# The down weights of a mixture of experts, loaded by halves of the partitions instead of halves of the rows

## The reference, cut to what matters

```
logits = h @ router_w + router_b
gates, top_i = softmax of the two largest logits, their experts
for e in range(8):
    g, u = split(h @ w_gu[e])               # w_gu[e]: 1024 x 7168
    y += combine[:, e] * ((silu(g) * u) @ w_down[e])   # w_down[e]: 3584 x 1024
```

## Time and profile before

| | |
|---|---|
| median of the runs | 1408.96 us |
| profiled execution | 1409.0 us |
| its span | 1407.3 us |
| TensorE busy | 1224.8 us (87%) |
| VectorE busy | 793.6 us (56%) |
| gate/up matmuls (L951) | 547.5 us busy |
| down matmuls (L963) | 282.4 us busy |
| copies `w_dn<-w_next` (L1626) | 280 of 1201 ns |
| moved by DMA | 460.19 MB, 327 GB/s over the span |
| chain that ended last | issue 64%, PE 26%, DMA 5% |

### The profile page before, as it was taken

How to read it: one execution, slowest core, us unless ns; L and a number is a source line. 1 busy time by engine, 2 the same in 40 slices (tenths; PEclk the granted TensorE clock), 3 DMA queues, 4 the chain that set the end, 5 groups by cost and what they waited for, 6 DMA issues and landing times.

```text
span 1407.3 us, 38408 instructions
## 1 busy us (share of the span) xinstructions
PE 1224.8 (87%) x15648; PEld 803.4 (57%) x15648; DVE 793.6 (56%) x1253; ACT 285.3 (20%) x567; POOL 41.2 (3%) x42
## 2 busy tenths in 40 slices
PE   4898998999998499878897987898798889888992
PEld 1456965888887466445553654455454546545651
DVE  0597846777774746545553654464454636545644
ACT  2005644333333321101110100111010101001111
POOL 1010000000000210000000000000000000000001
PEclk8899999999999599989998999999999989989996
DMA  9994121888899137999999999999999999999996
GB/s 339 391 363 153 58 91 30 288 296 293 294 343 364 60 116 287 397 397 397 386 400 396 390 397 400 399 393 397 398 400 397 397 397 383 400 396 397 392 400 207
DMA packets 184427, 460.19 MB, mean 327 GB/s; under 512 B 8480, under 2 KB 34128, under 8 KB 169936
## 3 DMA queue, kind: packets, MB, share of 16 engines
q1 hardware_dynamic: 169776, 403.72, 76.5%
q0 software_dynamic: 13952, 55.58, 10.6%
q10 hardware_dynamic: 672, 0.54, 0.1%
HBM read 455.74 MB, written 4.06 MB: 327 GB/s over the span
## 4 chain that ended last, share of the span: by engine, by line
issue 64%; PE 26%; DMA 5%; DVE 3%; ACT 1%; POOL 1%; SPq 0%; POOLq 0%; DVEq 0%; ACTq 0%
PE ps L640 4%; PE ps L816 4%; PE ps L768 2%; PE ps L770 2%; PE ps L769 2%; PE ps L758 2%; PE ps L700 2%; DMA wqkv<-in_attn_w_qkv 2%; DMA ada<-in_ada_w 1%; DMA f_raw<-in_ffn_w_gu 1%; PE ps L689 1%; PE ps L605 1%; PE ps L935 1%; DVE f_lo L1434 1%; PE ps L678 1%
## 5 line engine op out<-in xcount | busy, mean ns | idle before, releaser
L951 PE MATMUL ps<-w_gu,consts_sb 128*32 128x256 f32 x8960 | 547.5, 396 | 97.2 <-DMA w_gu<-in_moe_w_gu 91.2
L951 PEld LDWEIGHTS ps<-w_gu,consts_sb 128*32 128x32 f32 x8960 | 306.1, 113 | 312.8 <-DMA w_gu<-in_moe_w_gu 111.3
L1626 DVE COPY w_dn<-w_next 128x2048 f32<-128x2048 f32 x280 | 324.9, 1201 | 0.0
L963 PE MATMUL ps<-w_dn,consts_sb 128*32 128x256 f32 x4512 | 282.4, 390 | 2.1 <-DVE w_dn L1626 2.1
L963 PEld LDWEIGHTS ps<-w_dn,consts_sb 128*32 128x32 f32 x4512 | 158.4, 114 | 104.1 <-issue 19.6
L1208 ACT ACTIVATE consts_sb<-ps 128x128 f32<-128x128 f32 x140 | 38.8, 277 | 760.3 <-PE ps L951 760.3
L1613 DVE TENSOR_TENSOR consts_sb<-consts_sb,ps 128x128 f32<-128x128 f32 x140 | 55.0, 393 | 241.0 <-ACT consts_sb L1208 241.0
L1620 DVE TENSOR_TENSOR y_all<-y_all,ps 128x256 f32 x140 | 59.0, 421 | 179.4 <-PE ps L963 179.4
L1303 DVE SCALAR_TENSOR_TENSOR ada_acc<-ada,cols,ada_acc 128x512 f32<-128x512 f32 x140 | 105.0, 750 | 4.0
L1434 DVE TENSOR_TENSOR f_lo<-f_raw,f_hi 128x2048 fp32r<-128x2048 f32 x32 | 73.0, 2292 | 47.2 <-ACT f_hi L1104 46.1
L1104 ACT ACTIVATE f_hi<-f_raw 128x2048 fp32r<-128x2048 f32 x32 | 61.0, 1915 | 64.9 <-DMA f_raw<-in_ffn_w_gu 61.0
(11 more groups left out here) (226 smaller groups left out, 884.7 us busy)
## 6 DMA issues: line engine op xcount, KB each, us to landing
w_gu<-in_moe_w_gu SPq DMA_DIRECT2D x224, 1024.0 KB, 15.5
w_next<-in_moe_w_down SPq DMA_DIRECT2D x112, 1024.0 KB, 13.3
ada<-in_ada_w POOLq DMA_DIRECT2D x23, 2048.0 KB, 10.1
f_raw<-in_ffn_w_gu SPq DMA_DIRECT2D x44, 512.0 KB, 6.6
f_raw<-in_ffn_w_down SPq DMA_DIRECT2D x11, 1024.0 KB, 5.0
wqkv<-in_attn_w_qkv SPq DMA_DIRECT2D x3, 2048.0 KB, 19.6
wo_sb<-in_attn_w_o SPq DMA_DIRECT2D x1, 4096.0 KB, 23.6
ada_fourth<-in_ada_w POOLq DMA_DIRECT2D x1, 2048.0 KB, 29.4
```

The lines of the kernel that those rows point to most:

```text
L951: mm = pe.matmul(ps[UNIT * t:UNIT * t + UNIT, GU_BANK, 0:2 * W], x_cur[:, k, :], gate_up_columns(w_gu[x], half, kk, t), start=(k == 0), st ...
L963: mm = pe.matmul(ps[UNIT * t:UNIT * t + UNIT, Y_BANK, 0:OW], m_actT[:, q, :], w_dn[:, q, OW * t:OW * t + OW], start=(q == 0), stop=(q == 3))
L1626: dve.tensor_copy(w_dn[:, 2 * half:2 * half + 2, :], w_next[:, y, 2 * half:2 * half + 2, :]).then_inc(s[f"d_copied{half}"], 1)
```

## The change

The two DMAs of a down load no longer halve the rows but the partitions: the first writes partitions 0 to 63, the second 64 to 127, each partition's four rows in one piece of 16 KB. VectorE's copies are the same two (two rows of all 128 partitions each), and since each needs both DMAs, both waits come ahead of the first copy.

```diff
         def load_down(y, e, step):
             for half in range(2):
-                src = mdn_v[bass.ds(e, 1), bass.ds(step, 1), :, 2 * half:2 * half + 2, :]
-                sp.dma_start(w_next[:, y, 2 * half:2 * half + 2], src.rearrange("e s p q n -> p (e s q) n")
-                             ).then_inc(s[f"d_in{y}{half}"], 16)
+                rows = slice(P // 2 * half, P // 2 * half + P // 2)
+                src = mdn_v[bass.ds(e, 1), bass.ds(step, 1), rows, :, :]
+                sp.dma_start(w_next[rows, y], src.rearrange("e s p q n -> p (e s q) n")).then_inc(s[f"d_in{y}{half}"], 16)
...
             for half in range(2):
                 dve.wait_ge(s[f"d_in{y}{half}"], fills)
+            for half in range(2):
                 dve.tensor_copy(w_dn[:, 2 * half:2 * half + 2, :], w_next[:, y, 2 * half:2 * half + 2, :]
                                 ).then_inc(s[f"d_copied{half}"], 1)
```

## The result

The changed kernel took 1918.81 us (median of three runs, 1907.81 to 1928.93), 1.3621 times the time of before, interval 1.35 to 1.3742: 510 us slower. The prediction was 1659, range 1460 to 1725. The direction was right, about half of the size was missing.

A forecast was written before the change was run, and what follows sets the result against it. The prediction took the DMA weight stream to bound the mixture-of-experts stage. Added to 1409 us, 252.5 us for down loads at half rate less 2.1 us at the end, +250.4 us, gave 1659 us, range 1460 to 1725.

The forecast's parts named there:

- What bounds the stage: Mixture-of-experts stage: the DMA stream alone paces 53 steps of 15.73 us, 834 us from 541.87 us on.
- The pieces: Down loads: one 16 KB piece for two of 8 KB saves 0.03 us per DMA, 3.2 us over 106.
- The partitions, the main term: Down loads into half the partitions: two engines share one way, +2.38 us per DMA, 252.5 us over 53 steps.
- The waits: VectorE's merged wait costs 0; a TensorE wait of some 2.3 us at the down projection lies beside the stream.
- The ends: First six down DMAs cost 0; at the end the slower stream eats the last copy's cover, -2.1 us.
- the first rival, "engines out of step": Down loads: engines sharing a way drift apart and avoid collisions, 1534 or 1472 us; 16% for 1406 to 1600.
- The clause on running dry: In the stream, engines that get ahead run dry and start together again with the next DMA; no size given.
- a share well under 1: In the stage, a DMA share well under 1 would mean something other than the stream paces it.
- The sign for engines out of step, 330 to 380 GB/s: In the stage, a rate of 330 to 380 GB/s would mean the engines are out of step.
- a lower rate for each load by itself: Down loads at 193 or 188 GB/s, worse than half rate: 1717 or 1733 us; 7%, far end 3%.
- the clock rival: TensorE left at half clock throughout by longer stalls: 25.9 us a step, 1948 us; 2%.

The follow-up runs named there:

- both kernels with the wait: SP waits each step, before issuing the down pair, for the previous step's gate/up weights: changed kernel 1785.68 us, kernel before 1539.17 us.
- the bound: Changed kernel, SP waiting each step before the down pair for only the first half of the previous step's gate/up weights: 1678.80 us, ratio 1.1904.
- 1694: Changed kernel, SP waiting in one step of six, before the down pair, for the previous step's gate/up weights: 1693.91 us, ratio 1.2027.

## Why the prediction was wrong, step by step

*What bounds the stage: right.* The whole loss is in the stream of the stage, and what lies before and after it kept its length within 2 us.

*The pieces: small, as said, but the 3.2 us are not shown.* Over all partitions the pieces of 16 KB came with a gain of 3.4 us, in one DMA for two. With even and odd partitions, with the same pieces in two DMAs, nothing was gained (1.0012, 0.9998 to 1.0026).

*The partitions, the main term: right.* Two engines to one way, 2.38 us a down DMA, 252.5 us for 106. Engines kept in step pay 246.5 us (both kernels with the wait) to 269 us (the bound, against its own runs of before), that is 2.33 to 2.54 us a DMA, and the first loads of the changed kernel move at 211 GB/s against about 215 forecast. The choice of the 193 GB/s of the earlier trace rows over the 377 to 385 of the earlier trace rows was right; why those stores ran at 385 stays open.

*The waits: right.* The edit alone costs nothing, and the new wait at the down projection is there and lies beside the stream. With the bound, TensorE waits 210.7 us for gate and up weights and 76.4 at the down projection, 287 where some 300 were forecast.

*The ends: a small misreading.* The 11.2 us of the earlier trace rows are the median over the two loads of the last pair. By its last increment the pair had landed at 1376.80 us, so that the cover ahead of the copy was 0.65 us and not 2.1. After, the last increment comes at 1884.08 us and the copies begin at 1886.66, so that no cover was eaten. The term of -2.1 us is not borne out.

*The step that failed* is the one under the first rival, "engines out of step", and with it a term that the sum left as it was: the four gate and up DMAs of a step at 2.68 us each, whatever the down loads do. The prediction said that engines which part can only save ("one is in the lower half while the other is in the upper, and nothing collides"), and that any which get ahead "run dry and start together again", so that all stay near one step of 20.50 us.

Parting does not save. Once the engines are apart, the gate and up weights pay too: from 97 ns a piece to 134, with the engines full, and the step goes from 21.1 to 26.4 us. That such a piece then shares its way with the down piece of another engine fits these durations; the records name no way, so that it is not shown. The clause on running dry holds from 1058 us on, for fifteen engines, and fails for the sixteenth: it is not set back, stays 14 to 15 us behind for the rest of the stage and paces the stream, at a step of 26.2 us. The runs that hold the engines together (1786, 1694, 1679) against the one that doesn't (1919) show that the slip costs 240 to 263 us on top.

Of the prediction's own signs, a share well under 1 came only late: the rate was down to 249 GB/s while the share was 1.04. The sign for engines out of step, 330 to 380 GB/s, pointed the wrong way.

The range had no case for it: above 1725 the prediction had only a lower rate for each load by itself and the clock, at 3% and 2%. The 1948 of the clock rival is near the measured 1919 by number only: the granted clock was 0.74 to 0.85 in the stretches shown and not a half throughout, and one wait on SP takes 240 us away.

*What stays open.* Why an engine falls behind at all, and which. It isn't the order of the halves. In the packet records from 1200 to 1800 us some 6 pieces of 16 KB a step take 1.6 to 2.0 us, where the median is 1.28, and some 61 gate/up pieces a step take over 240 ns, where the median is 85; one engine has 8 and 128 of them a step. That would fit a late engine that meets two others on one way, but the records do not name the engine, so that it is not shown.

## What to carry to other kernels

If a load into SBUF has to be split, split it by rows, or by even and odd partitions, and not into 0 to 63 and 64 to 127. Where a DMA stream sets the end, look at the rate over the length of the stage and not only at its start. A rate that falls while the share stays full is the first sign here that engines have parted, a share that sinks the second; the spread of a load's sixteen increments tells it from a queue that runs empty (the wait in each step has a share of 0.93 and no spread). A wait that keeps the issue close behind the landings can then be worth far more than the overlap that it gives up.

## What the runs showed of the hardware that was not expected

- With loads over all ways the sixteen DMA engines stay within 0.5 to 2.0 us of each other over the whole stage (the spread of the sixteen increments, before and with even and odd partitions). With loads that collide nothing held them together: five fell 5 to 14 us behind, and later one 14 to 15 us while fifteen waited.
- Engines that have parted slow the loads over all partitions too: a gate/up piece of 2 KB took 134 ns in the mean, where it took 88 before and 92 with the engines held together.
- 64 partitions are enough for the full rate if they are every second one: the stage at 399 GB/s with even and odd partitions, where a load into one half moved at 211.
- Emptying the queue once a step costs 2.7 us (131 us over 48 waits).
- One load of 2 MB in pieces of 16 KB, for two of 1 MB in pieces of 8 KB, gains 0.2% here (0.998, 0.9967 to 0.9992).
